# Two attention mixers of a transformer block: the heads' score and value products issued in pairs, each head on its half of the TensorE array

## What is computed

```
proj = h @ w_in[l]                      # 256 x 2816
a_u, a_v, b_q, b_k, b_v, c_q, c_k, c_v = split(proj)
y_a = spatial_gating(a_u, a_v, ...)     # called gate_mix in the kernel
y_b = stick_breaking(b_q, b_k, b_v)     # 6 heads of 64
y_c = dilated_window(rope(c_q), rope(c_k), c_v)   # 6 heads of 64
y   = concatenate([y_a, y_b, y_c]) @ w_out[l]
```

## Time and profile before

| | |
|---|---|
| median of 3 runs | 961.06 us |
| the profiled execution | 966.07 us |
| its span | 964.2 us |
| PE busy | 926.5 us (96%) |
| DVE busy | 616.8 us (64%) |
| ACT busy | 497.6 us (52%) |
| GpSimd busy | 2.9 us |
| DMA, mean over the span | 183 GB/s |

### The profile page before, as it was taken

The page is one execution under the profiler, slowest core; times in us unless marked ns, Lnnn a source line. Parts: engine busy times, 40 slices in busy tenths (PEclk is TensorE's granted clock), DMA queues, the critical chain, the costliest instruction groups (busy, mean ns, idle before and its releaser), DMA issues.

```text
span 964.2 us, 18266 instructions
## 1 busy us (share of the span) xinstructions
PE 926.5 (96%) x7641; PEld 874.7 (91%) x7641; DVE 616.8 (64%) x976; ACT 497.6 (52%) x730; POOL 2.9 (0%) x6
## 2 busy tenths in 40 slices
PE   4799999899999999999999999999999999999997
PEld 2688877799999999877999999999999999999996
DVE  0575664677777677877665666557886765666654
ACT  3446762655555557675644433446556663443341
POOL 1000000000000000000000000000000000000000
PEclk9899999999999999999999999999999999999999
DMA  9997748474555668332375555555452645555531
GB/s 326 325 319 246 248 176 280 166 242 170 179 188 176 217 176 175 88 88 86 114 255 183 176 175 179 194 174 179 130 173 88 219 153 193 178 177 175 181 126 45
DMA packets 132463, 176.91 MB, mean 183 GB/s; under 512 B 19665, under 2 KB 112125, under 8 KB 132253
## 3 DMA queue, kind: packets, MB, share of 16 engines
q1 hardware_dynamic: 131756, 173.97, 55.1%
q10 hardware_dynamic: 624, 1.77, 0.6%
HBM read 174.68 MB, written 1.05 MB: 182 GB/s over the span
## 4 chain that ended last, share of the span: by engine, by line
PE 88%; DVE 5%; ACT 3%; DMA 2%; issue 1%; SPq 0%; DVEq 0%; ACTq 0%
PE psum L1565 26%; PE psum L1557 24%; PE psum L1558 24%; PE psum L1657 2%; DMA raw<-in_w_ada_dram 2%; DVE w_lo L939 1%; PE psum L1561 1%; PE psum L1562 1%; PE psum L1942 1%; PE psum L2063 1%; ACT w_hi L519 1%; PE psum L1997 1%; PE psum L2007 1%; PE psum L2018 1%; ACT arena L804 1%
## 5 line engine op out<-in xcount | busy, mean ns | idle before, releaser
L1557 PE MATMUL psum<-h_hi,w_hi 128*128 128x256 f32 x1352 | 333.4, 285 | 5.1 <-DVE h_lo L1098 4.4
L519 ACT ACTIVATE w_hi<-raw 128x2048 fp32r<-128x2048 f32 (+1 forms) x139 | 264.5, 1904 | 142.9 <-PE psum L1565 114.1
L1558 PE MATMUL psum<-h_lo,w_hi 128*128 128x256 f32 x1352 | 327.3, 280 | 0.0
L939 DVE TENSOR_TENSOR w_lo<-raw,w_hi 128x2048 fp32r<-128x2048 f32 (+1 forms) x139 | 313.3, 2278 | 16.7 <-ACT w_hi L519 16.7
L1557 PEld LDWEIGHTS psum<-h_hi,w_hi 128*128 128x128 f32 x1352 | 256.1, 189 | 16.1 <-issue 12.3
L1558 PEld LDWEIGHTS psum<-h_lo,w_hi 128*128 128x128 f32 x1352 | 256.1, 189 | 0.2
L1565 PE MATMUL psum<-h_hi,w_lo 128*128 128x256 f32 x1352 | 188.2, 280 | 0.3 <-DVE w_lo L939 0.3
L1557 PE MATMUL psum<-a_hi,w_hi 128*128 128x256 f32 x720 | 172.6, 280 | 1.4 <-DVE a_lo L1288 1.2
L1565 PEld LDWEIGHTS psum<-h_hi,w_lo 128*128 128x128 f32 x1352 | 172.0, 189 | 0.6 <-DVE w_lo L939 0.6
L1558 PE MATMUL psum<-a_lo,w_hi 128*128 128x256 f32 x720 | 172.0, 279 | 0.0
L1557 PEld LDWEIGHTS psum<-a_hi,w_hi 128*128 128x128 f32 x720 | 135.4, 188 | 2.0 <-issue 1.9
(11 more groups left out here) (272 smaller groups left out, 778.7 us busy)
## 6 DMA issues: line engine op xcount, KB each, us to landing
raw<-in_mlp_w_in_dram SPq DMA_DIRECT2D x32, 1024.0 KB, 5.6
raw<-in_mlp_w_out_dram SPq DMA_DIRECT2D x32, 1024.0 KB, 7.2
raw<-in_w_ada_dram SPq DMA_DIRECT2D x24, 1024.0 KB, 7.3
raw<-in_w_up_dram SPq DMA_DIRECT2D x22, 1024.0 KB, 5.1
raw<-in_gla_w_in_dram SPq DMA_DIRECT2D x12, 1024.0 KB, 5.4
raw<-in_w_down_dram SPq DMA_DIRECT2D x11, 1024.0 KB, 5.4
raw<-in_w_in_dram SPq DMA_DIRECT2D x10, 1024.0 KB, 8.5
raw<-in_w_out_dram SPq DMA_DIRECT2D x4, 1024.0 KB, 6.4
```

Source lines behind the costliest of these rows:

```text
L519: act.activation(halved(w_hi, m % SPLIT_SLOTS, SPLITS[m]), halved(raw, r % RAW_SLOTS, SPLITS[m]), ACT.Copy).then_inc(*mark("w_hi", m))
L939: dve.tensor_tensor(halved(w_lo, m % SPLIT_SLOTS, key), halved(raw, r % RAW_SLOTS, key), halved(w_hi, m % SPLIT_SLOTS, key).bitcast(F32), ...
L1557: pe.matmul(dst, high, both[0], start=start, stop=False, skip_group_check=True)
L1558: return pe.matmul(dst, high, both[1], start=False, stop=False, skip_group_check=True)
```

## The change

- `stick_a` and `win_a` on PE work on two heads at once, at the even h; the odd h issues nothing. A pair takes two banks together. Each head's products contract over its own 64 rows of query and key tiles: first the 256-column product of both heads, then the 128-column product of both.
- The zeroed copies, their clearing on GpSimd, and the split writes of ACT and DVE go; the queries are written once as a full tile (`bq_t`, `cq_t`).
- `values_out` makes both heads in one call, with the products of the two heads in turn: 256 columns of either, then 128 of either. It waits for both heads first.
- The list of steps changes in tails 7 to 9.

```diff
--- before.py
+++ after.py
@@ -152,9 +152,9 @@
                6: [("win_a", 3), ("stick_a", 0), ("stick_a", 1)],
-             7: [("win_a", 4), ("v_norm",), ("stick_b", 0), ("stick_b", 1), ("stick_a", 2)],
-             8: [("win_a", 5), ("stick_a", 3), ("stick_b", 2)],
-             9: [("win_b",), ("stick_a", 4), ("gate_mix",), ("stick_b", 3), ("stick_a", 5)],
+             7: [("win_a", 4), ("win_a", 5), ("v_norm",), ("stick_b", 0), ("stick_b", 1)],
+             8: [("stick_a", 2), ("stick_a", 3)],
+             9: [("stick_a", 4), ("stick_b", 2), ("win_b",), ("stick_b", 3), ("gate_mix",), ("stick_a", 5)],
              10: [("stick_b", 4), ("stick_b", 5), ("win_c", 0), ("win_c", 1), ("split", 1, 0), ("split", 1, 1),
                   ("stick_c", 0), ("win_c", 2), ("win_c", 3), ("win_d", 0), ("stick_c", 1), ("split", 1, 2),
                   ("win_c", 4), ("win_c", 5), ("win_d", 1), ("split", 1, 3), ("stick_c", 2), ("mod", 3),
@@ -329,9 +329,9 @@
 
 
         u_t, v_tok, v_nrm = area(0, 2), area(2, 2), area(4, 2)
-        bqz, bk_t = area(6, 6), area(12, 3)
+        bq_t, bk_t = area(6, 3), area(12, 3)
         vals = arena[:, 15 * S:21 * S].rearrange("p (t c) -> p t c", t=TT)
-        cqk, cqz, ck_t = area(21, 6), area(27, 6), area(33, 3)
+        cqk, cq_t, ck_t = area(21, 6), area(27, 3), area(33, 3)
         w_sp_r = arena[:, 0:2 * S].rearrange("p (g s) -> p g s", g=4)
         w_sp_t = arena[:, 46 * S:48 * S].rearrange("p (g s) -> p g s", g=4)
         angle = area(38, 6)
@@ -498,12 +498,6 @@
             sp.wait_ge(*at("out_landed", TT - 1, 1))
 
 
-        @block.gpsimd
-        def _(pool):
-            pool.memset(bqz, 0.0).then_inc(*mark("zeroed", 0))
-            pool.memset(cqz, 0.0).then_inc(*mark("zeroed", 1))
-
-
         @block.scalar
         def _(act):
             done = {"hi": 0}
@@ -660,12 +654,7 @@
                     elif n == IN_V:
                         copy(job, v_tok[:, m, :], ACT.Gelu_apprx_tanh)
                     elif n < 6 and t - 6 < 3:
-                        act.wait_ge(*at("job", *job))
-                        act.wait_ge(*at("zeroed", 0))
-                        act.activation(bqz[0:64, 2 * (t - 6), :], bank(*job)[0:64, 0:S], ACT.Copy, scale=0.125)\
-                            .then_inc(*mark("b_q", t - 6))
-                        act.activation(bqz[64:128, 2 * (t - 6) + 1, :], bank(*job)[64:128, 0:S], ACT.Copy,
-                                       scale=0.125).then_inc(*mark("act_read", *job))
+                        copy(job, bq_t[:, t - 6, :], scale=0.125)
                     elif n < 6:
                         copy(job, bk_t[:, t - 9, :])
                     else:
@@ -1125,15 +1114,8 @@
                 dve.tensor_tensor(work[:, 1, :], bank("rope", t)[:, 0:S], angle[:, 0, :], ALU.mult)\
                     .then_inc(*mark("dve_read", "rope", t))
                 dve.wait_ge(*at("dve_read", "rope", t))
-                if t < 3:
-                    dve.wait_ge(*at("zeroed", 1))
-                    dve.tensor_tensor(cqz[0:64, 2 * t, :], work[0:64, 0, :], work[0:64, 1, :], ALU.add)\
-                        .then_inc(*mark("roped", t, 1))
-                    dve.tensor_tensor(cqz[64:128, 2 * t + 1, :], work[64:128, 0, :], work[64:128, 1, :], ALU.add)\
-                        .then_inc(*mark("roped", t, 2))
-                else:
-                    dve.tensor_tensor(ck_t[:, t - 3, :], work[:, 0, :], work[:, 1, :], ALU.add)\
-                        .then_inc(*mark("roped", t, 2))
+                dst = cq_t[:, t, :] if t < 3 else ck_t[:, t - 3, :]
+                dve.tensor_tensor(dst, work[:, 0, :], work[:, 1, :], ALU.add).then_inc(*mark("roped", t, 2))
 
             def v_norm():
 
@@ -1739,12 +1721,18 @@
 
             def stick_a(h):
 
+                if h % 2:
+                    return
                 pe.wait_ge(*at("act_read", "in", 5, 1))
-                dst = take(pe, "stick", h)
-                k = bk_t[:, h // 2, :]
-                pe.matmul(dst[:, 0:S], k[:, 0:P], bqz[:, h, :], start=True, stop=False, skip_group_check=True)
-                pe.matmul(dst[:, S:SP3], k[:, P:S], bqz[:, h, P:S], start=False, stop=False, skip_group_check=True)\
-                    .then_inc(*mark("job", "stick", h))
+                dst = [take(pe, "stick", h + e) for e in range(2)]
+                k, q = bk_t[:, h // 2, :], bq_t[:, h // 2, :]
+                for e in range(2):
+                    half = slice(HD * e, HD * e + HD)
+                    pe.matmul(dst[e][:, 0:S], k[half, 0:P], q[half, :], start=True, stop=False, skip_group_check=True)
+                for e in range(2):
+                    half = slice(HD * e, HD * e + HD)
+                    pe.matmul(dst[e][:, S:SP3], k[half, P:S], q[half, P:S], start=False, stop=False, skip_group_check=True)\
+                        .then_inc(*mark("job", "stick", h + e))
 
             def stick_b(h):
 
@@ -1755,30 +1743,37 @@
                 pe.matmul(dst[:, S:SP3], cst("tail"), s[:, S:SP3], start=False, stop=True, skip_group_check=True)\
                     .then_inc(*mark("stick_tail", h))
 
-            def values_out(dst, h, column, prob):
-
-                o = 64 * (h % 2)
-                pe.matmul(dst[o:o + 64, 0:S], vals[:, 0, column:column + HD], prob[:, 0:S], start=True, stop=False,
-                          skip_group_check=True)
-                return pe.matmul(dst[o:o + 64, P:S], vals[:, 1, column:column + HD], prob[:, S:SP3], start=False,
-                                 stop=True, skip_group_check=True)
+            def values_out(dst, m, column, probs):
+
+                for t in range(TT):
+                    for e in range(2):
+                        c = column + (2 * m + e) * HD
+                        prob = probs[e][:, 0:S] if t == 0 else probs[e][:, S:SP3]
+                        ins = pe.matmul(dst[HD * e:HD * e + HD, t * P:S], vals[:, t, c:c + HD], prob, start=(t == 0),
+                                        stop=(t == 1), skip_group_check=True)
+                return ins
 
             def stick_c(m):
                 dst = take(pe, "stick_o", m)
-                for h in (2 * m, 2 * m + 1):
-                    pe.wait_ge(*at("stick_weight", h))
-                    pe.wait_ge(*at("act_read", "in", 10, 1))
-                    ins = values_out(dst, h, h * HD, stick(h))
-                ins.then_inc(*mark("job", "stick_o", m))
+                pe.wait_ge(*at("stick_weight", 2 * m + 1))
+                pe.wait_ge(*at("act_read", "in", 10, 1))
+                values_out(dst, m, 0, (stick(2 * m), stick(2 * m + 1))).then_inc(*mark("job", "stick_o", m))
 
             def win_a(h):
+
+                if h % 2:
+                    return
                 if h == 0:
                     pe.wait_ge(*at("roped", 5, 2))
-                dst = take(pe, "win", h)
-                pe.matmul(dst[:, 0:P], cqz[:, h, 0:P], ck_t[:, h // 2, 0:P], start=True, stop=True,
-                          skip_group_check=True)
-                pe.matmul(dst[:, P:SP3], cqz[:, h, P:S], ck_t[:, h // 2, :], start=True, stop=True,
-                          skip_group_check=True).then_inc(*mark("job", "win", h))
+                dst = [take(pe, "win", h + e) for e in range(2)]
+                k, q = ck_t[:, h // 2, :], cq_t[:, h // 2, :]
+                for e in range(2):
+                    half = slice(HD * e, HD * e + HD)
+                    pe.matmul(dst[e][:, P:SP3], q[half, P:S], k[half, :], start=True, stop=True, skip_group_check=True)
+                for e in range(2):
+                    half = slice(HD * e, HD * e + HD)
+                    pe.matmul(dst[e][:, 0:P], q[half, 0:P], k[half, 0:P], start=True, stop=True, skip_group_check=True)\
+                        .then_inc(*mark("job", "win", h + e))
 
             def win_c(h):
                 pe.wait_ge(*at("win_scaled", h, 1))
@@ -1789,10 +1784,8 @@
 
             def win_d(m):
                 dst = take(pe, "win_o", m)
-                for h in (2 * m, 2 * m + 1):
-                    pe.wait_ge(*at("act_read", "win_t", h))
-                    ins = values_out(dst, h, 6 * HD + h * HD, win_pt(h))
-                ins.then_inc(*mark("job", "win_o", m))
+                pe.wait_ge(*at("act_read", "win_t", 2 * m + 1))
+                values_out(dst, m, 6 * HD, (win_pt(2 * m), win_pt(2 * m + 1))).then_inc(*mark("job", "win_o", m))
 
             def project(kind, n):
                 if (kind, n) == ("out", 0):
```

## The result

| | before | after |
|---|---|---|
| median of 15 runs each | 961.35 us | 963.69 us |
| ratio, 95% interval | | 1.0023 (1.0013 to 1.0034) |
| the profiled execution | 966.07 us | 964.96 us |
| its span | 964.2 us | 963.1 us |

The forecast was 960.5 with a range of 957.2 to 963.4. The change is slower, within the 0.3% that were called no change but with an interval that leaves 1 out, and the time lies 0.3 us above the range.

A forecast was written before the change was run, and what follows sets the result against it. The prediction took PE, busy for 96% of the span, to bound the kernel. PE's own time and the old gap -3.9, two waits in tail 9 +2.8, tail 10 +0.5: -0.6, from 961.06 to 960.5 us, range 957.2 to 963.4.

The follow-up runs named there:

- experiment 2: The changed kernel with win_b moved behind stick_b(3) in tail 9; ratio to the kernel before 1.0000.
- 4: The changed kernel with the products with the values in their old order, both of one head, then both of the other; ratio to the kernel before 1.0033.
- 5: The changed kernel with a pair's scores issued head by head instead of in turn; ratio to the kernel before 1.0028.
- 10: The changed kernel with rows(2) and rows(3) ahead of the window pair in tail 4 and nothing else; ratio to the kernel before 1.0015.
- experiment 7: The changed kernel with the old list of steps in tails 7 to 9, except gate_mix behind stick_b(3); ratio to the kernel before 1.0068.
- 6: The changed kernel with gate_mix moved to tail 8 and rows(2), rows(3) ahead of tail 4's window pair; 959.03 us, ratio to the kernel before 0.9955.
- 9: The kernel before, with single heads and zeroed copies, given the changed list with gate_mix moved to tail 8; ratio to the kernel before 0.9989.

## What to carry to other kernels

Ask first whose queue carries the chain once the engine in question is shorter: here PE's gain beyond 93 us fell to a chain of ACT and DVE. When PE gets shorter ahead of a shared ring of buffers, walk through the ring again: for every take, name the reader of what lay there before and what stands in its queue. A wait of PE as long as these, 1.7 us and more, should be costed twice, once as time and once as a clock that may fall behind it; here the second was nearly half of the first. And before giving up a change that loses, move the step that waits: the same pairs went from 0.23% slower to 0.45% faster than before with three entries of a list in other places.

## What the runs showed of the hardware that was not expected

- A single gap of 1.72 us on PE in tail 9 was followed by 1.2 GHz (experiment 2), as were two of 1.8 to 1.9 and 0.75 to 1.2 us with 0.7 to 1.1 us of work between (the changed kernel, 4, 5, 10), and each of the gaps of 3.63 and 2.14 us in experiment 7. Gaps of 0.67, 0.73 and 0.21 us were not.
- The same gap doesn't always do it. The wait for an ada chunk near 150 us, 1.49 to 2.07 us, was followed by a fallen clock in the profiled executions of before (1.85) and of experiment 4 (2.07), and in none of the others, among them experiment 5 with 2.04 and 6 with 1.87. The wait of 1.7 us for DVE some 27 us later, the same in all twelve, was followed by one in experiments 6 and 9 alone. What tells these apart stays open, and so does whether tail 9's gaps would do it in every execution.
- In eleven of the twelve profiled executions the clock also fell for about 4 us near 445 or near 705. One profiled execution can so differ by 1.6 us from another of the same kernel; S, which leaves those places out, followed the medians better than the spans did.
- Products on different halves of rows run side by side in either order of issue (0.85 and 0.86 us for a pair).
